# The last expert's down projection in another order and other banks, and the end's vector and scatter work reordered

## The reference

```python
hdn = jax.nn.silu(xb @ w_gate[e]) * (xb @ w_up[e])     # 512 hidden channels
y   = hdn @ w_down[e]                                  # 1024 outputs, for the tokens of expert e
...
x = layer_norm(ALPHA * x + ffn, ln_moe_g, ln_moe_b)    # ffn: gate-weighted sum of a token's two experts
```

## Time and profile before

| | before |
|---|---|
| median of 3 runs | 1749.63 us (1748.44 to 1750.38) |
| the profiled execution's own time | 1747.1 us |
| its span | 1745.6 us |
| PE busy | 1643.5 us (94%) |
| DVE busy | 1086.3 us (62%) |
| ACT busy | 659.4 us (38%) |
| POOL busy | 338.4 us (19%) |
| granted TensorE clock, mean | 0.974 |

### The profile page before, as it was taken

How to read it: one execution, slowest core, us unless ns; L and a number is a source line. 1 busy time by engine, 2 the same in 40 slices (tenths; PEclk the granted TensorE clock), 3 DMA queues, 4 the chain that set the end, 5 groups by cost and what they waited for, 6 DMA issues and landing times. The chain is left out here.

```text
span 1745.6 us, 25478 instructions
## 1 busy us (share of the span) xinstructions
PE 1643.5 (94%) x9626; PEld 1427.8 (82%) x9626; DVE 1086.3 (62%) x1681; ACT 659.4 (38%) x922; POOL 338.4 (19%) x266
## 2 busy tenths in 40 slices
PE   8999999999999999999996649999999999999993
PEld 6888888888888888788885648999999999999982
DVE  5445866358673586834765666555566666666766
ACT  4234323143231433324333314344555455544440
POOL 1000024000160000600004012122323233233332
PEclk9999999999999999999998859999999999999997
DMA  7322435322463224432244824666777677777761
GB/s 230 97 73 73 157 109 194 97 73 79 139 217 97 72 73 169 158 133 73 73 145 163 320 79 147 190 213 214 237 247 244 213 226 249 252 229 241 255 192 56
DMA packets 120012, 283.64 MB, mean 162 GB/s; under 512 B 14256, under 2 KB 16432, under 8 KB 119888
## 3 DMA queue, kind: packets, MB, share of 16 engines
q1 hardware_dynamic: 92624, 192.81, 32.7%
q0 software_dynamic: 26688, 87.05, 16.8%
q10 hardware_dynamic: 576, 2.10, 0.3%
HBM read 236.96 MB, written 48.37 MB: 163 GB/s over the span
## 5 line engine op out<-in xcount | busy, mean ns | idle before, releaser
L492 DVE TENSOR_TENSOR mix_w_low<-mix_w_raw,mix_w_high 128x2048 fp32r<-128x2048 f32 x73 | 167.2, 2291 | 163.3 <-ACT mix_w_high L359 163.1
L742 PE MATMUL mix_acc<-mix_xT_high,mix_w_high 128*128 128x512 f32 x640 | 254.2, 397 | 0.6 <-DVE mix_w_low L492 0.6
L744 PE MATMUL mix_acc<-mix_xT_high,mix_w_low 128*128 128x512 f32 x640 | 250.1, 391 | 0.0
L743 PE MATMUL mix_acc<-mix_xT_low,mix_w_high 128*128 128x512 f32 x640 | 249.2, 389 | 0.0
L359 ACT ACTIVATE mix_w_high<-mix_w_raw 128x2048 fp32r<-128x2048 f32 x73 | 139.7, 1914 | 258.0 <-PE mix_acc L744 248.9
L1678 DVE TENSOR_TENSOR moe_gate_up_low<-kept_w_gate_up_raw,moe_gate_up_high 128x2048 fp32r<-128x2048 f32 x64 | 146.5, 2290 | 81.0 <-ACT moe_gate_up_high L1550 81.0
L2005 PE MATMUL moe_gate_psum<-moe_xT_high,moe_gate_up_high 128*128 128x288 f32 x512 | 154.1, 301 | 1.4 <-DVE moe_xT_low L1695 1.4
L2007 PE MATMUL moe_up_psum<-moe_xT_high,moe_gate_up_low 128*128 128x288 f32 x512 | 152.0, 297 | 0.0
L2006 PE MATMUL moe_up_psum<-moe_xT_low,moe_gate_up_high 128*128 128x288 f32 x512 | 151.8, 296 | 0.0
L2006 PE MATMUL moe_gate_psum<-moe_xT_low,moe_gate_up_high 128*128 128x288 f32 x512 | 151.7, 296 | 0.0
L2005 PE MATMUL moe_up_psum<-moe_xT_high,moe_gate_up_high 128*128 128x288 f32 x512 | 151.5, 296 | 0.0
(11 more groups left out here) (402 smaller groups left out, 3592.3 us busy)
## 6 DMA issues: line engine op xcount, KB each, us to landing
mix_w_raw<-in_w_in SPq DMA_DIRECT2D x57, 1024.0 KB, 5.3
kept_w_gate_up_raw<-in_w_gate SPq DMA_DIRECT2D x32, 1024.0 KB
kept_w_gate_up_raw<-in_w_up SPq DMA_DIRECT2D x32, 1024.0 KB
kept_w_down_raw<-in_w_down SPq DMA_DIRECT2D x32, 1024.0 KB, 10.1
mix_w_raw<-in_w_out SPq DMA_DIRECT2D x16, 1024.0 KB, 5.2
mix_x_rows<-in_x POOLq DMA_DIRECT2D x16, 512.0 KB, 6.6
kept_conv_or_residual<-in_x POOLq DMA_DIRECT2D x16, 512.0 KB, 5.1
x<-kept_conv_or_residual POOLq DMA_DIRECT2D x16, 512.0 KB, 3.7
```

The lines of the kernel that those rows point to most:

```text
L492: dve.tensor_tensor(wl[:, stage % 2], raw[:, stage % 2], wh[:, stage % 2].bitcast(F32), ALU.subtract).then_inc(split_l, 1)
L742: pe.matmul(out, ah, bh, start=first, stop=False)
L743: pe.matmul(out, ah, bl, start=False, stop=False)
L744: return pe.matmul(out, al, bh, start=False, stop=last)
```

## The change

TensorE's last expert runs A, then U, then B in two halves: B's first half goes into `pg[0]` (the bank of gate), its second half into `pu[0]` (the bank of up), each with all four hidden chunks, and the quarters' averaging matmul stands between the two. B no longer waits for VectorE's sum of A. On VectorE the list norm of expert 14's first tile moves ahead of the last expert's first hidden chunk; sums go A, U, B's first half, the quarters, B's second half; each half is added and then measured before the next; norms go U, B, A, and then the three list tiles. GpSimd issues the three scatters back first, after all three variances (`end_var`), then U's, B's and A's stores, and the lists' last. The core of the diff:

```diff
+        end_ps = (pg[0], pu[0])
...
-                list_store(r, LAST)
...
-XX                    wait_apart(pool, idle, end_normed, r * COLS + n + 1)
-                    end_store(r, n, k, to, most, END_OUT[k], index, end_stored)
+                wait_apart(pool, idle, end_var, r * COLS + COLS)
                 for k, to, most in ((U, quarter_rows, (S + 4 * P) * QUARTERS - 1), (A, acc_dram, S + 4 * P - 1),
                                     (B, acc_dram, S + 4 * P - 1)):
-                    end_store(r, n, k, to, most, END_IN[k], back_i[:, k:k + 1], end_stored)
+                    end_store(to, most, END_IN[k], back_i[:, k:k + 1])
+                for n, (k, to, most, index) in enumerate(((U, out_quarters, S * QUARTERS - 1, last_i[:, LAST:]),
+                                                          (B, out, S - 1, scatter_i[:, c + 1:c + 2]),
+                                                          (A, out, S - 1, scatter_i[:, c:c + 1]))):
+                    wait_apart(pool, idle, end_normed, r * COLS + n + 1)
+                    end_store(to, most, END_OUT[k], index)
+                list_store(r, LAST)
...
-                for n, k in enumerate((U, A, B)):
+                for n, k in enumerate((A, U, B)):
                     end_rstd_of(r, n, k)
...
+            def end_add(r, k, q):
+                width = DQ if k == U else BANK
+                part = END_IN[k][:, q * BANK:q * BANK + width]
+                from_ps = px[1][:, 0:DQ] if k == U else (py, end_ps)[k][q][:]
+                c = COLS * LAST + k
+                scale = last[:, 1, LAST:] if k == U else gate[:, c:c + 1]
+                own.step(dve.scalar_tensor_tensor(out=part, in0=from_ps, scalar=scale, in1=part,
+                                                  op0=ALU.mult, op1=ALU.add))
+                wait_apart(dve, idle, *own.due(r))
+                own.step(dve.bn_stats(end_stats[:, k, q], part))
...
+                    if e == LAST:
+                        row_norm(r, LAST - 1, 0, 1)
                     hidden(r, e, 0)
...
-                    row_norm(r, e - 1)
+                    row_norm(r, e - 1, 1 if e == LAST else 0)
...
                 row_stats(r, LAST)
+                end_sums(r, A)
                 end_sums(r, U)
+                dve.wait_ge(end_half, r + 1)
+                dve.wait_ge(end_in[B], r * 16 + 16)
+                end_add(r, B, 0)
                 end_quarters(r)
-                end_norm(r, 0, U)
-                end_sums(r, A)
+                end_sums(r, B)
+                end_norm(r, 1, U)
+                end_norm(r, 2, B)
+                end_norm(r, 0, A)
                 row_norm(r, LAST)
-                end_norm(r, 1, A)
-                end_sums(r, B)
-                end_norm(r, 2, B)
...
+            def down_end(r, q):
+                s = slice(q * BANK, (q + 1) * BANK)
+                for c in range(FC):
+                    ins = three(end_ps[q][:], hTh[:, c, AT[B]], hTl[:, c, AT[B]], dh[:, c, s], dl[:, c, s],
+                                c == 0, c == FC - 1)
+                ins.then_inc((end_half, b_used)[q], 1)
...
+                        down(r, e, A)
                         down_last(r, e)
-                        down(r, e, A)
+                        pe.wait_ge(hid_done, r * (NE * FC) + NE * FC - 1)
+                        down_end(r, 0)
                         pe.wait_ge(end_sq_done, r + 1)
                         pe.matmul(px[0][:, 0:2], same[:], end_sq[:], start=True, stop=True).then_inc(end_mean, 1)
-                        down(r, e, B)
+                        down_end(r, 1)
```

More of the change, by code:

```diff
@@ L1384, in experts @@
         end_var, end_rs, end_normed = sem("end_var_ready"), sem("end_rstd_ready"), sem("end_rows_normed")
-        end_sum, end_mean, end_sq_done = sem("end_rows_summed"), sem("end_quarters_averaged"), sem("end_squares_ready")
-        end_stored = sem("end_rows_stored")
+        end_mean, end_sq_done = sem("end_quarters_averaged"), sem("end_squares_ready")
+        end_stored, end_half = sem("end_rows_stored"), sem("end_first_half_in_psum")
         act_own = sem("act_own")
@@ L1487, in end_rows, with end_store @@
                                             in_offset=bass.IndirectOffsetOnAxis(ap=index, axis=0)).then_inc(end_in[k], 16)
-            def end_store(r, n, k, to, most, rows, index, sem):
+            def end_store(to, most, rows, index):
                 pool.indirect_dma_start(out=to, out_offset=bass.IndirectOffsetOnAxis(ap=index, axis=0),
-                                        in_=rows, in_offset=None, bounds_check=most, oob_is_err=False).then_inc(sem, 16)
+                                        in_=rows, in_offset=None, bounds_check=most, oob_is_err=False)\
+                    .then_inc(end_stored, 16)
             n_rounds = trips(pool)
@@ L1669, in _ @@
         def _(dve):
-            DVE_TURN = 97 + NE * FC
+            DVE_TURN = 104 + NE * FC
             own = Order(dve, dve_own, DVE_TURN)
@@ L1882, in row_stats, with row_norm @@
                 ins.then_inc(var_done, 1)
-            def row_norm(r, e):
+            def row_norm(r, e, first=0, end=RTILES):
                 if e not in BATCH:
@@ L1889, in row_norm @@
                 dve.wait_ge(rs_done, r * len(BATCHES) + BATCHES.index(e) + 1)
-                for n, i in enumerate(BATCH[e]):
+                for n, i in list(enumerate(BATCH[e]))[first:end]:
                     rows = R[row_tile(i)]
@@ L1896, in row_norm @@
                                              op0=ALU.mult, op1=ALU.add).then_inc(normed, 1)
-            def end_sums(r, k):
[L1900 to L1904, removed]
-                else:
[L1906 to L1915, removed]
+            def end_add(r, k, q):
[8 more added lines that the diff above has]
+                own.step(dve.bn_stats(end_stats[:, k, q], part))
+            def end_sums(r, k):
+                if k == B:
+                    dve.wait_ge(b_used, r * NE + NE)
+                    end_add(r, B, 1)
+                else:
+                    dve.wait_ge((a_used, None, u_used)[k], r * NE + NE)
+                    dve.wait_ge(end_in[k], r * 16 + 16)
+                    for q in range(2 if k == A else 1):
+                        end_add(r, k, q)
                 wait_apart(dve, idle, *own.due(r))
-                ins = dve.bn_aggr(end_mv[:, k], end_stats[:, k, 0:len(parts)])
+                ins = dve.bn_aggr(end_mv[:, k], end_stats[:, k, 0:1 if k == U else 2])
                 if k != U:
@@ L2040, in gate_up @@
                 ins.then_inc(gu_used, 1)
+            def down_end(r, q):
[4 more added lines that the diff above has]
+                ins.then_inc((end_half, b_used)[q], 1)
             def down(r, e, k):
                 if k == B:
-                    if e < LAST:
-                        for done in (y_act, y_dve):
-                            pe.wait_ge(done, r * (2 * LAST) + 2 * e + 1)
-                    else:
-                        pe.wait_ge(end_sum, r * COLS + 2)
+                    for done in (y_act, y_dve):
+                        pe.wait_ge(done, r * (2 * LAST) + 2 * e + 1)
                 elif e:
```

4 lines of the change are left out of this document (removed).

## The result

| | before | changed |
|---|---|---|
| median | 1750.01 us (4 runs, 1748.44 to 1751.10) | 1739.91 us (4 runs, 1739.26 to 1741.62) |
| ratio | | 0.9948, 95% interval 0.9936 to 0.9960 |
| the profiled execution | 1747.1 us, span 1745.6 | 1741.62 us, span 1740.1 |
| all runs of this study | 1748.5 us (72 runs) | 1741.3 us (14 runs) |

The change makes the kernel faster, by 10.1 us in the first comparison and by 7.2 us over all runs. The traces of the first comparison differ by only 5.5 us, so a common mark is needed. I use the start of the last `gate_up` matmul, 1699.88 in the earlier trace rows and 1701.95 here; what follows it I call **the end**. It took 45.7 us before and takes 38.2 us now: 7.6 us less.

What follows compares the result with a forecast made beforehand. From 1700 us on VectorE's stream, then GpSimd's issues, bound the kernel. Stream gain 4.1 us, last issue 8.0 us earlier, longer tail and 0.2 us for list rows gave 6.3 us: 1743.3 us, range 1741.0 to 1746.5.

Steps and rivals of the forecast that it cites:

- Start of VectorE's stream: One list tile of expert 14 moved ahead lets the list statistics start 1.99 us sooner, at 1702.48.
- the list rows: Rows the list statistics need may land late: 0.2 us assumed; as a rival up to 1.99 us, chance 8%.
- TensorE: A follows gate_up at 1700.0, ends 1705.7; U's block ends 1707.6, B's halves 1710.4 and 1714.9.
- VectorE's waits: At the end, 4.15 us of waits for others vanish; 1.10 us for B's second half is new.
- added wait for an own result: VectorE waiting for its own result in the sums: 0.16 us each, 0.90 us for A, B and U together.
- Stream end: VectorE's last norm ends at 1730.40 instead of 1734.54, a gain of 4.1 us.
- GpSimd: Issues keep pace with VectorE's norms; the last list store starts at 1731.27, 8.0 us earlier than the last issue before.
- The slower rival: GpSimd's nine issues, slowed beside two-operand VectorE passes, become the bound: 1752.5 us, chance 5%.
- Its limit of 1.7 us: Time per GpSimd issue from which that slowing begins to matter at the end.
- The tail: From last issue's start to span's end: 6.33 us plus 1.5 us for a store with data, 7.8 us.
- From the span to the median: The 6.3 us gain, reckoned on a 1745.6 us span, was taken unchanged off the 1749.63 us median.

Runs made afterwards that it cites:

- B in A's banks: Changed kernel with B's halves in the banks of A, behind a wait for A's variance; 1744.02 us, ratio 0.9966 to the kernel before.
- before, scatters ahead: Kernel before with only the three scatters back put ahead of B's store, behind the third variance; 1748.11 us, ratio 0.9998.
- mean last: Changed kernel with the averaging matmul behind B's second half, and sums, norms and stores reordered; run twice, 1740.63 and 1739.71 us.
- scatters back last: Changed kernel with the three scatters back issued last, as before the change; 1744.34 us, ratio 0.9978 to the kernel before.
- lists first: Changed kernel with the three list tiles normed and stored before the norms of U, B and A; 1741.92 us, ratio 0.9958.

## Why the prediction was right in its way and wrong in its size

*Start of VectorE's stream:* right. Forecast 2.6 us after the mark plus 0.2 for the list rows; measured 2.80.

*TensorE:* right. From the mark, A was to start at 0.1, U's block at 5.8, B's first half at 7.7; measured 0.13, 5.78 and 7.64. The gap before the mean was 1.3 us (forecast 1.2), at full clock.

*VectorE's waits:* right. The three waits are gone, the wait for B's second half is 1.01 us (forecast 1.1). An added wait for an own result costs 0.16 us, except one of 0.50 behind the sum of B's first half. That one stayed in every version with this order, also with B in A's banks, so the bank isn't its cause; no run explains it. Stream end 30.8 us after the mark, forecast 30.7.

*GpSimd:* right. It kept pace: the last two list stores waited 1.26 and 1.35 us for VectorE. The slower rival, issues beside two-operand passes, showed only singly: 2.05 us for one store of the changed kernel, 1.87 for one scatter of "before, scatters ahead", 1.76 for one store in each trace of "mean last". The prediction read 1.17 us beside the norms and 0.97 alone as the price of such a pass. By the traces that holds for stores that had waited for a norm; most issues that follow one another beside the same passes took 0.97 to 1.03 us, as alone. Its limit of 1.7 us "an issue" is, by its own sum, the time from one start to the next, so about 1.4 us for the issue itself. The last issue starts 7.7 us earlier from the mark, forecast 7.8.

*The tail:* this step failed. The prediction said "Now the last one carries 512 KB" and added 1.5 us to 6.33. The tail was 6.46 us: the third tile of the last list holds no rows with these inputs, so the last store is as empty as the scatters back were. The size of the term was nearly right where it applies, 1.1 to 1.3 us (tails of 7.56, 7.56 and 7.76 against 6.33 to 6.51). Its condition was false. The kernel before could have shown it: its third list store is the row at 1726.69 in the earlier trace rows, and I never looked at the traffic behind it:

```profile
1728.00:1729.00 1.00, 0.00 (x0) 0.00 (x0) 1.00 (x3) 0.00 (x0) 0.84 (x1) 0.50 0.06 1
1729.00:1730.00 1.00, 0.00 (x0) 0.00 (x0) 0.97 (x2) 0.00 (x0) 0.70 (x2) 0.50 0.03 1
```

Two microseconds behind that issue, where the traffic of a store with data stands, there is 1 GB/s. Without the term the same sum gives a gain of 7.8 us, against 7.6 by the ends.

*From the span to the median:* this step is what put the result outside the range. Without the tail's term the forecast would have been 1741.8 us, and 1739.91 still lies 1.9 below that. The gain was set under a median of three runs, and I had taken such a median's own scatter (the three runs: 1748.44 to 1750.38) for nothing in the range. The measured gains of the same pair of kernels were 10.1, 7.5 and 5.3 us. The first is 2.5 us more than the ends give; the part ahead of the mark moves by more than that from trace to trace, so I take it for chance. What makes the first 50 us and the routing vary was not tried. The 1741.3 us over all runs do lie inside the range, but partly by luck: over all runs the kernel before has 1748.5 us, 1.1 under the median that the gain was taken from, and the tail's term was wrong all the same.

## What to carry to other kernels

The streams of this reordering could be priced to 0.2 us from one trace, by walking each instruction by instruction, as long as the clock stayed up; where it fell, the same way of reckoning was 1.5 to 1.6 us short. For every issue that becomes the last, look in the trace whether any traffic follows it: an indirect store whose indices lie beyond the bound costs the queue its second but not the tail its microsecond. Compare traces from a mark just ahead of the edit, and give the range of a small gain the scatter of the medians as well. Where TensorE waits for a small result in the middle of a block, a pause of 2.5 us can cost twice, once as a wait and once as a low clock behind it; move the small matmul behind the block, or the work that delays its input ahead.

## What the runs showed of the hardware

- Pauses of TensorE of 1.2 to 1.6 us left the granted clock at 1.00 in seven traces; pauses of 2.45 and 2.50 us, one trace each, had it at 0.54 and 0.51 in the stretch behind them. In the kernel before the pause of 3.69 us stayed at 1.00 throughout and the clock fell only after TensorE had resumed. The Trainium skill's page "TensorE: Matmul & The Clock Gate" (HAM oscillation) warns of longer pauses than these; by the traces these two matter too.
- An indirect scatter whose rows all lie beyond the bound took 0.98 to 1.0 us to issue, as one with data does, and the span ended 6.3 to 6.5 us after it, against 7.6 to 7.8 us for one with 0.5 MB. The profile gives 2.1 us from issue to landing for empty ones ("scatters back last" and "before, scatters ahead") and 3.3 to 3.4 for full ones ("before, scatters ahead" and "lists first"). "DMA: Bandwidth & Descriptors" of the Trainium skill (anatomy of one DMA) has a fixed part of about 2.0 us and a part by bytes; the traces agree.
- An issue of GpSimd beside VectorE's norms took 1.0 to 1.2 us nearly always, but 1.87 us for one scatter back, 2.05 us for one end store of the changed kernel (0.98 in its next trace) and 1.76 us for one end store in both traces of "mean last". Why these is open.
